# Two weight halves per run of products from the mixing stage on, first-group steps moved, and products of ones at the start of a Trainium2 decoder-layer kernel

## Chip, cores and metric

The kernel runs on one core of one Trainium2 chip. The metric is the device time of one execution in microseconds (us), and a version's time is the median of its runs. The engines are called TensorE (PE, with its weight loads as PEld), VectorE (DVE), ScalarE (ACT), GpSimd (POOL) and SyncE (SP).

## What is computed

One hybrid decoder layer on 256 tokens of width 2048, all in float32. The cut reference:

```python
h = rms_norm(x, norm_mix); proj = h @ w_in            # u, v, q/k/v, z, beta, a, gates
y_a = u * (causal_chunk_mix(rms_norm(v)) + bias)      # gMLP, u and v after GELU
q, k, v = split(silu(causal_conv4(dn_qkv)))
beta, g = sigmoid(dn_beta), -exp(a_log) * softplus(dn_a + dt_bias)
o = gated_delta_rule(q, k, v, g, beta)                # 16 heads of 128, chunked
y_b = rms_norm(o) * silu(z)
merged = gate_a * (y_a @ w_branch_a) + gate_b * (y_b @ w_branch_b)
x = x + merged @ w_out
x = x + (silu(f_gate) * f_up) @ w_down                # SwiGLU, width 5632
x = x + sigmoid(rms_norm(x) @ w_ple_gate) * (p @ w_ple_proj)
return rms_norm(x, norm_final)
```

## The kernel before, in words

**Halves and phases.** All weight matrices are streamed as "halves" of 512 KB (128 x 1024 float32), 604 of them, through rings of four buffers: `raw` as loaded, `whi` (rounded to fp32r) and `wlo` (the rest). A half in feature layout holds 4 k-tiles by 2 column tiles of 128 x 128. For each half, SyncE issues one load (`load_half`, L272, waits until the low part of the half four earlier is made); ScalarE makes the high part (`split_hi`, L278, waits for the load and until the half four earlier is used up, semaphore `half_used`); VectorE makes the low part (`split_lo`, L288); TensorE runs `use_half` (L309). ScalarE and VectorE work three halves ahead (`LEAD`).

**One half on TensorE.** In feature layout the weight is the stationary operand. `use_half` waits for the high part, issues 8 products of 512 columns (`times_high`, L299: high and low activation side by side), waits for the low part and issues 8 products of 256 columns (`times_low`, L304), the last of which counts up `half_used`. In the phases v, proj and most of ple (`rows=True`) the activation is stationary and all products have 512 columns (L319, L324). `gemm` (L584) runs the halves of one output block into one of two accumulators and, through `after`, runs further TensorE steps behind a named half.

**Phases** (`PLAN`, L65): v (16 halves), qkvz (4 head groups of 32 halves, group 0 unrolled, 1 to 3 in a loop), u (16), mix (4 passes of 28; one pass is two blocks of 4, 4, 2 and 4 halves: two gates, branch a, branch b), out (2 passes of 16), ffn (11 passes of 16), down (2 passes of 44, blocks of 11), proj (4), ple (32). The first pass of mix, out, ffn and down is unrolled, the others are loops.

**The written order.** The small work of the delta rule hangs on half numbers, in a table for each engine: `FIRST` for group 0, `START` for the others, `FINISH` for the end of a group, which runs during the next one (TensorE L789 to L792, ScalarE L1120 to L1125, VectorE L1565 to L1571). A step runs behind the half of its number on its engine. Each engine runs its own list in order, so a step that waits holds up the splits or products behind it.

**Group 0.** VectorE scans the log decays (`sum_g`, L1595). ScalarE makes `tails` (L1137, an Exp into `bg`), stores the decays by DMA (`g_store`) and loads them back (`g_load`). TensorE transposes `bg` (`tok_columns`, L608, behind half 2, waits for `tails`); VectorE copies the result (`tok_copy`, L1606), in the middle of which it waits for ScalarE's `tok_exp` (L1142). The keys: two convolution steps (L1424, L1427), `silu_k` on ScalarE (L1019, L1021), `k_columns` on TensorE (L644, behind half 11), normalisation, `gram_m` (L659), `make_negm` (L1492), `store_m` and `load_m` (L1089, L1097, a round trip through DRAM on ScalarE's queue), then GpSimd's `invert` (L484), whose result goes through `store_x` and `load_diag` (L1105, L1113) to `merge32_a` (L701) in the next group. `transpose_k` (L671) and `scale_k` (L1507) must be over before `gram_q` (L680), which reuses their PSUM tile. The v branch ends in `v_norm` and `v_scale` (L1618, L1627).

**First mixing block.** `mix(0)` needs `ya` and `yb` as high and low parts: `ya_high`, `yb_high` on ScalarE (L1223, L1211), `ya_low`, `yb_low` on VectorE (L1692, L1665), placed by the two tables `YS` (L1241, L1708). TensorE waits for both `ya` parts before branch a (L844) and for all four `yb` parts before branch b (L846).

**Start.** TensorE waits for six constants (L621) and the first part of x, ScalarE for `cols` (L1011). Then ScalarE splits x and squares it, GpSimd adds the squares (L475), and TensorE sums them (`first_sum`, L617).

## Time and profile before

| what | value |
|---|---|
| median of 3 runs (lowest, highest) | 1848.9 us (1844.15, 1851.63) |
| profiled execution | 1843.6 us |
| its span, first to last instruction | 1842.0 us |
| mean granted TensorE clock | 0.997 |
| busy: PE, DVE, ACT, POOL | 98%, 64%, 48%, 14% |
| HBM rate over the span | 180 GB/s |

Each instruction row tells its start in us from the start of the span, its duration, the engine (PEld is a weight load, a q behind an engine's name its DMA queue), the line in the kernel, the operation, and the tiles as out<-in with their shapes. Neighbouring equal instructions are merged, with their count as x8. Matmuls overlap, so the spacing of their starts tells their pace and not their duration. A number in brackets is idle time of the engine before the row, with what ended it.

### The profile page before, as it was taken

Reading aid. Unit: us, or ns where it says so; the run is one execution under the profiler, and the core shown is the slowest. Engines: PE = TensorE matmul, PEld = TensorE weight load, DVE = VectorE, ACT = ScalarE, POOL = GpSimd, SP = SyncE. Lnnn points to the kernel's source line nnn. Section 1 sums busy time; section 2 is a strip of 40 time slices with the busy share of each in tenths; the row PEclk is TensorE's granted clock in tenths of the full one; section 3 lists DMA queues with packets and bytes.
Section 4 is the critical chain, followed back from the end, with each engine's and each line's share of the span. In section 5 each row is a group of like instructions: output and inputs, shape, how many; then the busy total and the mean of one; then the engine's idle time right before and its main releaser. Section 6 shows DMA issues by size and latency. Waiting matters only on the chain.

```text
span 1842.0 us, 29968 instructions
## 1 busy us (share of the span) xinstructions
PE 1806.9 (98%) x10742; PEld 1585.7 (86%) x10742; DVE 1177.2 (64%) x1403; ACT 893.3 (48%) x1039; POOL 249.5 (14%) x367
## 2 busy tenths in 40 slices
PE   8899999999999999999999999999999999999998
PEld 6688888888889788888888888888888888888887
DVE  6487697776866656566676655566656555555656
ACT  6645454455455544444444444444444444343455
POOL 4007143070431000000011000000000000000002
PEclk9999999999999999999999999999999999999999
DMA  7455546455465555655555555555555556565653
GB/s 250 139 174 168 159 141 196 123 173 155 150 197 172 182 196 182 194 181 194 172 191 197 193 185 192 183 182 183 190 193 191 189 183 195 183 195 182 217 175 134
DMA packets 103867, 332.94 MB, mean 181 GB/s; under 512 B 23185, under 2 KB 23329, under 8 KB 103521
## 3 DMA queue, kind: packets, MB, share of 16 engines
q1 hardware_dynamic: 88592, 320.57, 53.5%
q10 hardware_dynamic: 14096, 5.07, 1.2%
q0 software_dynamic: 1088, 6.03, 0.9%
q8 instruction: 65, 1.06, 0.2%
q14 instruction: 26, 0.20, 0.0%
HBM read 328.46 MB, written 3.16 MB: 180 GB/s over the span
## 4 chain that ended last, share of the span: by engine, by line
PE 91%; DVE 4%; issue 2%; ACT 2%; DVEq 0%; DMA 0%; ACTq 0%; SPq 0%
PE acc L301 52%; PE acc L306 27%; PE acc L319 4%; PE acc L324 2%; DVE wlo L294 1%; PE ps L635 1%; ACT whi L286 1%; PE acc L901 0%; PE acc L900 0%; PE acc L899 0%; PE ps L687 0%; PE ps L601 0%; PE ps L641 0%; DVE negm L1498 0%; DVE conv_q L1427 0%
## 5 line engine op out<-in xcount | busy, mean ns | idle before, releaser
L294 DVE TENSOR_TENSOR wlo<-raw,whi 128x1024 fp32r<-128x1024 f32 x604 | 755.4, 1268 | 449.2 <-ACT whi L286 445.8
L286 ACT ACTIVATE whi<-raw 128x1024 fp32r<-128x1024 f32 x604 | 625.9, 1055 | 511.1 <-PE acc L306 445.4
L301 PE MATMUL acc<-ax,whi 128*128 128x512 f32 x3072 | 777.9, 395 | 2.9 <-ACT whi L286 2.0
L301 PEld LDWEIGHTS acc<-ax,whi 128*128 128x128 f32 x3072 | 553.3, 189 | 105.4 <-issue 3.0
L306 PEld LDWEIGHTS acc<-ax,wlo 128*128 128x128 f32 x3072 | 419.0, 190 | 30.4
L306 PE MATMUL acc<-ax,wlo 128*128 128x256 f32 x3072 | 428.1, 282 | 0.0
L301 PE MATMUL acc<-fx,whi 128*128 128x512 f32 x704 | 176.3, 392 | 0.0
L301 PEld LDWEIGHTS acc<-fx,whi 128*128 128x128 f32 x704 | 126.6, 189 | 22.6
L967 ACT ACTIVATE t<-acc 128x512 f32<-128x512 f32 x80 | 47.8, 598 | 134.7 <-PE acc L306 131.3
L549 POOL TENSOR_TENSOR sqsum<-sqsum,t 128x512 f32<-128x512 f32 x16 | 22.1, 1381 | 637.6 <-ACT t L1282 637.6
L1395 DVE TENSOR_TENSOR t<-acc,t 128x512 f32<-128x512 f32 x80 | 55.3, 691 | 78.1 <-ACT t L967 77.7
L306 PEld LDWEIGHTS acc<-fx,wlo 128*128 128x128 f32 x704 | 96.0, 190 | 6.9
L306 PE MATMUL acc<-fx,wlo 128*128 128x256 f32 x704 | 98.2, 282 | 0.0
L319 PE MATMUL acc<-whi,ax 128*128 128x512 f32 x320 | 81.9, 399 | 8.3 <-ACT whi L286 8.3
L557 POOL TENSOR_TENSOR t<-t,R 128x512 f32<-128x512 f32 x22 | 28.6, 1298 | 451.7 <-ACT t L1295 451.7
L493 POOL TENSOR_TENSOR blk_t<-blk_m,blk_x 128x60 f32<-128x60 f32 (+24 forms) x124 | 58.4, 471 | 173.9 <-DMA blk_m<-inv_in 164.6
L319 PEld LDWEIGHTS acc<-whi,ax 128*128 128x128 f32 x320 | 61.2, 193 | 21.0 <-issue 8.2
L495 POOL TENSOR_TENSOR blk_x<-blk_x,blk_t 128x60 f32<-128x60 f32 (+24 forms) x124 | 70.0, 565 | 9.7
L301 PE MATMUL acc<-yb,whi 128*128 128x512 f32 x256 | 64.2, 393 | 1.9 <-DVE yb L1668 1.9
L301 PE MATMUL acc<-mx,whi 128*128 128x512 f32 x256 | 64.1, 392 | 0.0
L301 PEld LDWEIGHTS acc<-yb,whi 128*128 128x128 f32 x256 | 46.0, 189 | 10.3 <-DVE yb L1668 2.1
L301 PEld LDWEIGHTS acc<-mx,whi 128*128 128x128 f32 x256 | 46.0, 189 | 8.2
(269 smaller groups left out, 1366.8 us busy)
## 6 DMA issues: line engine op xcount, KB each, us to landing
raw<-in_win SPq DMA_DIRECT2D x224, 512.0 KB, 3.6
raw<-in_wgu SPq DMA_DIRECT2D x176, 512.0 KB, 4.1
raw<-in_wd SPq DMA_DIRECT2D x88, 512.0 KB, 4.1
raw<-in_wb SPq DMA_DIRECT2D x32, 512.0 KB, 4.2
raw<-in_wo SPq DMA_DIRECT2D x32, 512.0 KB, 4.3
raw<-in_wpg SPq DMA_DIRECT2D x32, 512.0 KB, 3.9
raw<-in_wa SPq DMA_DIRECT2D x16, 512.0 KB, 4.6
blk_m<-inv_in ACTq DMA_DIRECT2D x16, 128.0 KB, 3.0
```

Source lines behind the costliest of these rows:

```text
L286: nc.scalar.activation(whi[:, s], raw[:, s], ACT.Copy).then_inc(hi_done, 1)
L294: nc.vector.tensor_tensor(wlo[:, s], raw[:, s], whi[:, s].bitcast(F32), ALU.subtract).then_inc(lo_done, 1)
L301: nc.tensor.matmul(o, whi[:, s, kt, m * P:(m + 1) * P], x[:, k].rearrange("p q n -> p (q n)"), start=begin, stop=False, skip_group_check=True)
L306: return nc.tensor.matmul(o[:, 0:SEQ], wlo[:, s, kt, m * P:(m + 1) * P], x[:, k, 0], start=False, stop=end, skip_group_check=True)
L319: nc.tensor.matmul(into[buf][:, m], x[:, WIDE_K * h + kt, q, m * P:(m + 1) * P], whi_w[:, s, kt], start=first and kt == 0 and q == 0, stop ...
L324: mm = nc.tensor.matmul(into[buf][:, m], x[:, WIDE_K * h + kt, 0, m * P:(m + 1) * P], wlo_w[:, s, kt], start=False, stop=last and kt == WI ...
L493: chain(g.tensor_tensor(tmp, blk_m[:, j + 1:32, j:j + 1].to_broadcast([P, r, c]), blk_x[:, j:j + 1, 0:c].to_broadcast([P, r, c]), ALU.mult ...
L495: chain(g.tensor_tensor(blk_x[:, j + 1:32, 0:c], blk_x[:, j + 1:32, 0:c], tmp, ALU.add), v + 3 + 2 * j)
L549: g.tensor_tensor(sqsum[:], sqsum[:], piece(t[1], q % 2), ALU.add).then_inc(s["added"], 1)
L557: g.tensor_tensor(piece(t[1], j), piece(t[0], j), over(R[:], 2), ALU.mult).then_inc(ff_gate, 1)
L967: f(dst, accv[buf][:, :, 1], ACT.Copy).then_inc(low_taken, 1)
L1395: v.tensor_tensor(dst, accv[buf][:, :, 0], dst, ALU.add).then_inc(part_summed, 1)
```

## The change

It has four parts.

1. `use_pair` and `gemm_pairs`: two halves per run, high products of both (16), then low products of both (16). They are used in all of mix but three blocks of its first pass, and in the loop passes of out, ffn and down. Blocks with an odd number of halves end with a single one.
2. Group 0: `tok_columns` from half 2 to 5, `gram_q` from 22 to 23, `q_columns` from 24 to 25, `transpose_v` from 27 to 28; on ScalarE `tails` from 2 to 3, `tok_exp` from 4 to 6, the root for v from 6 to 8; on VectorE `tok_copy` from 3 to 6, `v_scale` from 7 to 9.
3. First mixing block: the first high and low part of `yb` are made in phase u, the others and those of `ya` one place earlier, and TensorE waits for each part of `ya` and `yb` just ahead of the half that reads it.
4. Start: 16 products of 64 columns of ones on TensorE, ahead of all else, and a Copy of one column of ones on ScalarE ahead of its wait for `cols`.

```diff
+WARM = 16
+    def use_pair(pe, phase, i, n, buf, first, last, h, x):
+        for p in range(2):
+            pe.wait_ge(hi_done, half_of(phase, i, n + p) + 1)
+            for kt in range(HALF_K):
+                for m in range(2):
+                    times_high(acc[buf][:, m], (n + p) % RING, kt, m, x, HALF_K * (h + p) + kt, first and p == 0 and kt == 0)
+        for p in range(2):
+            pe.wait_ge(lo_done, half_of(phase, i, n + p) + 1)
+            for kt in range(HALF_K):
+                for m in range(2):
+                    mm = times_low(acc[buf][:, m], (n + p) % RING, kt, m, x, HALF_K * (h + p) + kt,
+                                   last and p == 1 and kt == HALF_K - 1)
+            mm.then_inc(half_used, 1)
...
+            def gemm_pairs(phase, i, n0, halves, buf, use, x):
+                acc_free(pe, phase, i, buf, use)
+                for n in range(0, halves - 1, 2):
+                    use_pair(pe, phase, i, n0 + n, buf, n == 0, n + 2 == halves, n, x)
+                if halves % 2:
+                    use_half(pe, phase, i, n0 + halves - 1, buf, False, True, halves - 1, x)
...
+            pe.wait_ge(consts_made, 1)
+            for n in range(WARM):
+                mm(psf[1][:, 64 * n:64 * n + 64], ones[:], ones[:, 0:64], start=True, stop=True)
             pe.wait_ge(consts_made, 6)
...
-            FIRST = {2: tok_columns, 11: k_columns, 14: k_rows, 16: gram_m, 19: transpose_k, 22: gram_q, 24: q_columns, 27: transpose_v}
+            FIRST = {5: tok_columns, 11: k_columns, 14: k_rows, 16: gram_m, 19: transpose_k, 23: gram_q, 25: q_columns, 28: transpose_v}
...
             def mix(i, after=None):
                 for b in range(2):
-                    gemm("mix", i, MIX * b, HID, 0, 2 * b, ax, after=after if b == 0 else None)
-                    gemm("mix", i, MIX * b + HID, HID, 1, 2 * b, ax)
-                    pe.wait_ge(ya_lo, 2)
-                    gemm("mix", i, MIX * b + 2 * HID, HGM, 0, 2 * b + 1, ya)
-                    pe.wait_ge(yb_lo, NGROUPS)
-                    gemm("mix", i, MIX * b + 2 * HID + HGM, HID, 1, 2 * b + 1, yb)
+                    if after and b == 0:
+                        gemm("mix", i, MIX * b, HID, 0, 2 * b, ax, after=after)
+                    else:
+                        gemm_pairs("mix", i, MIX * b, HID, 0, 2 * b, ax)
+                    gemm_pairs("mix", i, MIX * b + HID, HID, 1, 2 * b, ax)
+                    if after and b == 0:
+                        pe.wait_ge(ya_lo, 1)
+                        gemm("mix", i, 2 * HID, HGM, 0, 1, ya, after={0: operand_ready(ya_lo, 2)})
+                        pe.wait_ge(yb_lo, 1)
+                        gemm("mix", i, 2 * HID + HGM, HID, 1, 1, yb, after={h: operand_ready(yb_lo, h + 2) for h in range(HID - 1)})
+                    else:
+                        gemm_pairs("mix", i, MIX * b + 2 * HID, HGM, 0, 2 * b + 1, ya)
+                        gemm_pairs("mix", i, MIX * b + 2 * HID + HGM, HID, 1, 2 * b + 1, yb)
...
-                    gemm("out", i, b * HID, HID, b % 2, b // 2, mx)
+                    gemm_pairs("out", i, b * HID, HID, b % 2, b // 2, mx)
...
-                    gemm("ffn", i, b * HID, HID, b % 2, b // 2, ax)
+                    gemm_pairs("ffn", i, b * HID, HID, b % 2, b // 2, ax)
...
-                    gemm("down", i, b * HFF, HFF, b % 2, b // 2, fx)
+                    gemm_pairs("down", i, b * HFF, HFF, b % 2, b // 2, fx)
...
+            act.wait_ge(consts_made, 1)
+            f(preload[:, 0:1], ones[:, 0:1], ACT.Copy)
             act.wait_ge(cols_in, 16)
...
                 if n == 2:
+                    g_store(0)
+                if n == 3:
                     tails()
-                    g_store(0)
                 if n == 4:
-                    tok_exp()
                     g_load(0)
                 if n == 6:
+                    tok_exp()
+                if n == 8:
                     act.wait_ge(v_mean, 3)
                     f(vrms[:], vrms[:], ACT.Sqrt).then_inc(v_root, 1)
...
+                if n == 14:
+                    yb_high(0)
...
-            YS = {0: (lambda: yb_high(0),), 1: (lambda: yb_high(1),), 2: (lambda: yb_high(2),), 5: (lambda: ya_high(0),),
+            YS = {0: (lambda: yb_high(1),), 1: (lambda: yb_high(2),), 5: (lambda: ya_high(0),),
                   6: (lambda: ya_high(1),), 7: (lambda: yb_high(3),)}
...
-                if n == 3:
+                if n == 6:
                     tok_copy()
...
-                if n == 7:
+                if n == 9:
                     v_scale()
...
                     o_scale(NGROUPS - 1)
+                    yb_low(0)
...
-            YS = {0: (lambda: yb_low(0),), 1: (lambda: norm_o(NGROUPS - 1),), 2: (lambda: yb_low(1),), 3: (sv_bias,),
-                  4: (lambda: ya_mult(0), lambda: ya_mult(1)), 6: (lambda: ya_low(0),), 7: (lambda: ya_low(1),),
-                  8: (lambda: yb_low(2),), 9: (lambda: yb_low(3),)}
+            YS = {0: (lambda: yb_low(1),), 1: (lambda: norm_o(NGROUPS - 1),), 3: (sv_bias,),
+                  4: (lambda: ya_mult(0), lambda: ya_mult(1)), 5: (lambda: ya_low(0),), 6: (lambda: ya_low(1),),
+                  7: (lambda: yb_low(2),), 8: (lambda: yb_low(3),)}
```

## Rows read from the trace of the kernel before

**Rows 1.** The page: the span, and each engine's busy time.
```profile
span 1842.0 us, 29968 instructions
PE 1806.9 (98%) x10742; PEld 1585.7 (86%) x10742; DVE 1177.2 (64%) x1403; ACT 893.3 (48%) x1039; POOL 249.5 (14%) x367
```

**Rows 2.** Waits of TensorE: who waited for whom, us in total, times, longest.
```profile
...
PE ps L614 <- ACT bg L1140: 7.3, 1, 7.3
PE ps L687 <- DVE kbeg L1510: 2.6, 1, 2.6
...
PE acc L301 <- DVE ya L1694: 1.9, 1, 1.9
PE acc L301 <- DVE yb L1668: 1.9, 1, 1.9
...
```

**Rows 3.** Timeline, 70 to 84 us: ScalarE and TensorE around the gate transposes.
```profile
...
76.37 1.06 ACT L286 ACTIVATE whi<-raw 128x1024 fp32r<-128x1024 f32 x1
...
78.74 0.40 ACT L1140 ACTIVATE bg<-bg 16x128 f32<-16x128 f32 x1
...
79.45 3.52 PE L301 MATMUL acc<-ax,whi 128*128 128x512 f32 x8
...
```

**Rows 4.** Timeline, 85 to 107 us: the chain to the key lengths.
```profile
...
85.98 0.69 DVE L1395 TENSOR_TENSOR pre<-acc,pre 128x512 f32<-128x512 f32 x1
...
99.76 2.46 DVE L1427 SCALAR_TENSOR_TENSOR conv_k<-pre,cols,conv_k 128x256 f32<-128x256 f32 x6
...
104.25 1.06 ACT L1021 ACTIVATE t<-conv_k 128x1024 f32<-128x1024 f32 x1
...
106.10 1.84 PE L635 MATMUL ps<-ones,t 128*128 128x1 f32 x16
...
```

**Rows 5.** Timeline, 128 to 146 us: the chain to the query gram.
```profile
...
128.30 2.15 DVE L1498 SCALAR_TENSOR_TENSOR negm<-ps,tok,negm 128x128 f32<-128x128 f32 x8
...
135.91 1.74 ACTq L1102 DMA_DIRECT2D blk_m<-inv_in  x4
...
145.80 2.02 PE L687 MATMUL ps<-conv_q,kn 128*128 128x128 f32 x16 [2.63 <-DVE kbeg L1510]
...
```

**Rows 6.** Timeline, 178 to 193 us: from GpSimd's inversion to the first merge.
```profile
...
178.17 1.48 POOL L497 COPY blk_xT<-blk_x 128x256 f32<-128x256 f32 x1 [0.17 <-POOL blk_x L495]
...
181.32 2.65 ACTq L1110 DMA_DIRECT2D inv_out<-blk_xT  x4
...
188.74 0.41 ACTq L1117 DMA_DIRECT2D diagT<-inv_out  x1
...
192.29 1.09 PE L709 MATMUL ps<-diagT,negm 32*32 32x32 f32 x32
...
```

**Rows 7.** Timeline of VectorE in the first mixing block: the first low part of ya.
```profile
...
605.46 1.22 DVE L1694 TENSOR_TENSOR ya<-ytmp,ya 128x1024 fp32r<-128x1024 f32 x1
...
```

**Rows 8.** Timeline of TensorE in ffn: one half and the start of the next.
```profile
...
1201.51 2.00 PE L301 MATMUL acc<-ax,whi 128*128 128x512 f32 x8
1203.35 1.11 PE L306 MATMUL acc<-ax,wlo 128*128 128x256 f32 x8
1204.30 2.00 PE L301 MATMUL acc<-ax,whi 128*128 128x512 f32 x8
...
```

**Rows 9.** Timeline of TensorE in ple, where every product has 512 columns.
```profile
...
1772.33 1.98 PE L319 MATMUL acc<-whi,ax 128*128 128x512 f32 x8
1774.14 1.07 PE L324 MATMUL acc<-wlo,ax 128*128 128x512 f32 x4
...
```

**Rows 10.** Timeline of the first 36 us: the cold start and what paces it.
```profile
...
8.25 3.75 PE L319 MATMUL acc<-whi,ax 128*128 128x512 f32 x8 [8.25 <-ACT whi L286]
...
33.90 3.88 ACT L286 ACTIVATE whi<-raw 128x1024 fp32r<-128x1024 f32 x4
...
35.67 1.98 PE L319 MATMUL acc<-whi,ax 128*128 128x512 f32 x8
...
```

**Rows 11.** The page: the costliest group, VectorE's low parts.
```profile
...
L294 DVE TENSOR_TENSOR wlo<-raw,whi 128x1024 fp32r<-128x1024 f32 x604 | 755.4, 1268 | 449.2 <-ACT whi L286 445.8
...
```

More of the change, by code:

```diff
@@ L838, in _, with operand_ready @@
                 gemm("u", 0, p * HID, HID, p % 2, p // 2, ax, after=last_steps(p * HID, HID))
+            def operand_ready(done, last):
+                return lambda: pe.wait_ge(done, last)
             def mix(i, after=None):
                 for b in range(2):
-                    gemm("mix", i, MIX * b, HID, 0, 2 * b, ax, after=after if b == 0 else None)
-                    gemm("mix", i, MIX * b + HID, HID, 1, 2 * b, ax)
-                    pe.wait_ge(ya_lo, 2)
-                    gemm("mix", i, MIX * b + 2 * HID, HGM, 0, 2 * b + 1, ya)
-                    pe.wait_ge(yb_lo, NGROUPS)
-                    gemm("mix", i, MIX * b + 2 * HID + HGM, HID, 1, 2 * b + 1, yb)
+                    if after and b == 0:
[11 more added lines that the diff above has]
+                        gemm_pairs("mix", i, MIX * b + 2 * HID + HGM, HID, 1, 2 * b + 1, yb)
             mix(0, after={0: lambda: turn_o(NGROUPS - 1), 2: spatial})
@@ L851, in _ @@
                 mix(i)
-            def operand_ready(done, last):
-                return lambda: pe.wait_ge(done, last)
             pe.wait_ge(mix_lo, 6)
```

## The prediction

> **What bounds the kernel now.** I read the page first. TensorE is busy for 1806.9 of 1842.0 us [rows 1], and no other engine comes near, so time is won only where TensorE waits or where its products come further apart than they need to. The waits of TensorE come second: four of them touch this change, 7.3, 2.6, 1.9 and 1.9 us [rows 2], 13.7 us together. Then the timelines around each, to see what is late next, and last the pace in the long loops. There a half takes 2.79 us, 1.84 for its 8 wide products and 0.95 for its 8 narrow ones [rows 8]. That is 0.230 and 0.119 us a product. Where wide products follow wide ones, 8 take 1.81 us, 0.226 each [rows 9]. So a wide run behind a narrow one costs some 0.025 us more than its products.
>
> **Part 1, two halves per run.** Nothing is added or removed; 159 pairs are formed (51 in mix, 8 in out, 80 in ffn, 20 in down). Each pair has one turn from narrow to wide less.
> - Gain: 0.025 us per pair, 4.0 us in all. Against it, the first narrow product behind a wide one may be quicker than the others: at 0.12 each, 8 would take 0.96 and they take 0.95 [rows 8]; a pair loses that once, up to 0.01. That leaves 0.015, or 2.4 us.
> - Bounds: 0.025 a pair (4.0 us) if the turn alone costs. If a narrow run of twice the length leaves twice the loss behind it, the turn costs the same per half and only the 0.01 is left, 1.6 us slower. I take 2.4, since the loss in rows 8 stands in the first products behind the turn and I see it as a fixed cost.
> - What hides the rest: in a pair `half_used` of the first half comes at 2 x 1.84 + 0.95 = 4.63 us instead of 2.79, so ScalarE may write that ring slot 1.84 us later. Its split (1.06) and VectorE's (1.27 [rows 11]) start three halves, 8.4 us, ahead. Tightest are the loops of out and down, where VectorE does two adds, a product and a low part (0.69 each [rows 4]) at each block's end and ScalarE two more operations, all ahead of the next split. Worked through from the end of a block: split and low part of the late slot until 1.5 us after it, three VectorE steps to 3.8, two of ScalarE's to 5.1, the split to 6.1; TensorE asks for it at 5.57 + 1.84 = 7.4. 1.3 us of cover stay. SyncE's loads wait for the same low parts and have a half more.
>
> *By a page.* In the Trainium skill, "TensorE: Matmul & The Clock Gate", section "Back-to-back issue gap", the spacing follows from the column count alone, with a small constant. By that rule order costs nothing and this part gives 0 instead of 2.4 us. The trace does not quite agree (0.230 against 0.226 for the same 512 columns).
>
> **Part 2, group 0.** This carries most of the sum, and its chain has four steps.
> - *The gate transposes.* TensorE ends half 2 at 71.8 us, waits 7.3 us for `tails`, which ends at 78.74 + 0.40 = 79.1, and then runs at the lower of its two clock levels (1.2 GHz): 8 wide products take 3.52 instead of 2.00 us [rows 3, 8]. That is 7.3 + 1.5 = 8.8 us. Behind half 5 the step comes 3 x 2.79 = 8.4 us later, at 80.2; `tails` is put behind one more split, so it ends at 80.1. Half 5 needs the split that ends at 77.4 [rows 3] and would start at 77.4. Both just fit: 8.8 us are free so far.
> - *The key lengths*, not moved, are late next. VectorE works from 85.98 to 102.2 without a gap up to the second key convolution, ScalarE's square ends at 105.3 and TensorE starts at 106.1 [rows 4]: 0.8 us of slack against 8.8 of advance. But the chain moves too. VectorE's stretch can begin when ScalarE has copied the first block, right behind `tails`: 80.1 + 0.6, so at 80.9. It loses `v_scale` (some 1.4 us, two passes of 1024 columns, which is what a low part is by size) and gets the token copies with their wait for `tok_exp` (some 1.6, being about ten short steps): 16.4 us instead of 16.2, so it ends at 97.3. ScalarE's two passes take it to 99.6. TensorE gets there at 97.3 and waits 2.3 us; a wait of 2.6 [rows 5] is followed by products at full pace, so the clock stays. Gain here: 106.1 - 99.6 = 6.5 us.
> - *The query gram.* From there on VectorE has no gap to close and stays 5.6 us ahead of before, TensorE 6.5. The chain `make_negm`, store, load, query SiLU, low parts to `scale_k` [rows 5] moves by 5.6. One half later, TensorE asks for it 2.8 us later: 2.8 - 0.9 = 1.9 of the 2.6 us go, 8.4 in all. `q_columns` and `transpose_v` only follow, one half later, at their old price.
> - *The inversion.* It starts with `load_m` [rows 5], so GpSimd too is 5.6 us early and ends at 179.65 - 5.6 = 174.0. ScalarE would store the result at 181.3 - 8.4 = 172.9 and now waits for it until 174.1, 7.2 us earlier than before; the DMA round trip to the first merge (181.3 to 192.3 [rows 6]) keeps its 11 us, and behind the waiting ScalarE stand its splits and block copy, so VectorE comes no earlier either. The gain falls to 7.3 us and is kept, since everything behind is paced by TensorE.
>
> Part 2 gives 7.3 us; its bounds are 8.4 (the inversion hidden) and 2.6 (the key chain doesn't move: 0.7 there and 1.9 at the gram).
>
> **Part 3, first mixing block.** Both waits are 1.9 us [rows 2]. The first `ya` part is ready at 605.46 + 1.22 = 606.7 [rows 7]; a weight's low part and the second `ya` part follow, some 2.3 us more, to 609.0, which is 1.9 behind TensorE: it wants `ya` at 607.1 and the second part only a half later. In the new order both come one low part earlier. Of `yb` the first is ready in phase u, the second and third long before, the fourth is wanted three halves later. The restart behind each wait goes with it, some 0.1 us. Cover: ScalarE and VectorE, for which nothing but order changes. Gain 4.0 us, bounds 3.8 and 4.2.
>
> **Part 4, start.** The first 8 wide products take 3.75 instead of 1.98 us [rows 10], at the lower clock level. If the products of ones lift the clock, TensorE is early, but it soon waits: ScalarE's split that ends at 33.9 + 1.05 = 34.95, itself paced by GpSimd's adds, feeds the products of 35.67 [rows 10]. So the gain is 0 to 0.7 us. The ones end some 4 us ahead of the first real product, which speaks against it; I take 0.3. The Copy brings ScalarE's table load forward, under the wait for the first weights: nothing.
>
> **Sum.** 2.4 + 7.3 + 4.0 + 0.3 = 14.0 us, or 1843.6 - 14.0 = 1829.6 us for the profiled execution. That one lies 5.3 us under the median of 1848.9, so I predict 1848.9 - 14.0 = 1834.9 us. What a measurement of this kernel can tell from no change is about 0.5%, 9.2 us.
>
> **The rivals.**
> - *The wait moves over.* The key chain doesn't come forward (ScalarE stuck in `tok_exp` behind VectorE, and VectorE in the same stretch as before). For it: 0.8 us of slack now, and VectorE with no gap from 86 to 102 us [rows 4]. Against it: VectorE's stretch starts when ScalarE lets it, and that is 5 us earlier. Part 2 gives 2.6, the sum 9.3, the time 1839.6 us. 19%, half of it under the bound of 9.2.
> - *The pairs give nothing.* By rows 8 and 9 this is a matter of 0.015 us a pair, close to the resolution of the rows. Sum 11.6, time 1837.3 us; with the loss of 1.6, 1838.9. 18%. This is the page's rule above.
> - *The pairs starve TensorE: slower.* Place: the split behind each block's end, where 1.3 us of cover stay. If ring slots freed 1.84 us later, with two loads bunched, make it late, TensorE waits once in each of the 77 paired blocks. It decides once the delay passes 1.3 + 14.0 / 77 = 1.5 us; at 1.3 + 0.3 it costs 23 us, and the time is 1848.9 - 14.0 + 23.1 = 1858.0 us. For it: the ring has only four slots. Against it: no wait in these loops is among TensorE's now [rows 2], and splits and low parts fill 2.3 of a half's 2.8 us on two engines. 6%.
> - *Nothing visible.* The median of other executions lies elsewhere than the profile, by up to 5 us, and small losses add up: sum 6 us, time 1842.9. 7%.
>
> **How the numbers follow.** My forecast has 50%, its own range 1831 to 1838. The range of 8 in 10 reaches from the best case (4.0 + 8.4 + 4.2 + 0.7 = 17.3 us, with some scatter of the median: 1829.0) to the case with 6 us gained, 1843.0. Faster by over 0.5%: nearly all of the forecast (47 of 50), 15 of the second rival's 18 and 9 of the first's 19 points: 71 of 100, which I take down to 66 for scatter of both medians. Slower by over 0.5%: 6. Within: 28.
>
> **What would show it.** Right: no wait at the gate transposes, and one of 2 to 3 us in front of the key-length products (L635) with `silu_k`'s square just ahead; the first merge in group 1 some 7 us earlier than 192.3; no waits for `ya` and `yb`; in the loops 16 wide and 16 narrow products per 5.57 us instead of 5.59. Wrong: a wait of over 6 us at the key lengths, pairs that take 5.59 us or more, any wait for `whi` in out, ffn or down, or a new wait in front of the first merges that eats more than 2 us.

## The result and the profile after

| what | before | changed |
|---|---|---|
| median (lowest, highest) | 1849.99 us (1844.15, 1851.63), 4 runs | 1826.07 us (1825.33, 1826.44), 4 runs |
| ratio, 95% interval | | 0.9883 (0.9870 to 0.9896) |
| profiled execution, span | 1843.6, 1842.0 us | 1825.33, 1823.7 us |

The change takes 1.2% off (1.1% in a later set, below). The direction was right, the forecast of 1834.9 us too small a gain, and the result lies 2.9 us below the range of 1829.0 to 1843.0.

The page of the changed kernel, its first lines and two of its queues:

```profile
span 1823.7 us, 30031 instructions
...
PE 1807.9 (99%) x10774; PEld 1590.6 (87%) x10774; DVE 1165.3 (64%) x1403; ACT 884.2 (48%) x1040; POOL 251.4 (14%) x367
...
q1 hardware_dynamic: 88592, 320.57, 54.0%
...
q8 instruction: 48, 0.79, 0.2%
...
```

TensorE has 32 more instructions of each kind than in [rows 1]: each of the 16 products of ones is recorded as two. The last line matters later. It is the queue that the page calls "instruction": it brings the program's own code, in 48 loads of some 16 KB (0.79 MB / 48). The page of before has 65 there.

The waits of TensorE in the changed kernel, which answer to [rows 2]:

```profile
PE ps L646 <- POOL ones L465: 1.2, 1, 1.2
PE acc L320 <- ACT whi L287: 1.0, 2, 0.7
PE ps L661 <- ACT t L1056: 1.0, 1, 1.0
PE ps L856 <- DVE oT L1601: 1.0, 1, 1.0
PE acc L302 <- ACTq L1192: 0.9, 1, 0.9
...
PE ps L760 <- DVE invT L1564: 0.6, 1, 0.6
...
```

All four waits of [rows 2] are gone. Three of about 1 us stand for them: ahead of half 4 of group 0 (L302, ACTq), at the key lengths (L661), and a new one in the first mixing block (L856).

To see where the time came from, take the start of the same step in both traces and subtract. A difference that stays the same from one step to the next means that nothing happened between them.

| step on TensorE | before, us | changed, us | gained so far | the part |
|---|---|---|---|---|
| end of stage v (first beta product) | 47.56 | 47.71 | -0.15 | start |
| key lengths | 106.10 | 99.59 | 6.51 | group 0 |
| first merge, group 1 | 192.29 | 183.80 | 8.49 | group 0 |
| first merge, group 2 | 308.07 | 298.40 | 9.67 | in no part |
| first merge, group 3 | 424.90 | 412.99 | 11.91 | in no part |
| first merge, in u | 539.50 | 527.58 | 11.92 | |
| second block of the first mixing pass | 628.00 | 612.87 | 15.13 | mixing order |
| proj | 1729.45 | 1711.17 | 18.28 | pairs |
| end | 1841.96 | 1823.70 | 18.26 | |

So by the traces: start -0.2, group 0 8.6, mixing order 3.2, pairs 3.1. With the start counted in, these are 14.8 us, against the 14.0 forecast. The other 3.4 us are gained between the merges of groups 1 and 3, where the change alters not one instruction. There TensorE goes from the last half of a pass of the loop of groups to the first half of the next. In before, the timeline of TensorE around the two back jumps shows:

```profile
291.13 2.10 PE L301 MATMUL acc<-ax,whi 128*128 128x512 f32 x8 [0.93 <-issue]
...
407.95 2.10 PE L301 MATMUL acc<-ax,whi 128*128 128x512 f32 x8 [1.96 <-ACT whi L286]
...
```

and in the changed kernel the halves at the second back jump follow each other every 2.8 us:

```profile
401.72 2.00 PE L302 MATMUL acc<-ax,whi 128*128 128x512 f32 x8
403.56 1.12 PE L307 MATMUL acc<-ax,wlo 128*128 128x256 f32 x8
404.52 2.00 PE L302 MATMUL acc<-ax,whi 128*128 128x512 f32 x8
406.36 1.11 PE L307 MATMUL acc<-ax,wlo 128*128 128x256 f32 x8
407.31 2.00 PE L302 MATMUL acc<-ax,whi 128*128 128x512 f32 x8
...
```

A back jump is where TensorE goes from the end of the loop's body to its start. The time from one first merge to the next holds one of them: 115.8 us (group 1 to 2) and 116.8 (2 to 3) in before, 114.6 for both in the changed kernel.

**Group 0.** The changed kernel at the gate transposes (L637) and the key lengths (L661), the answer to [rows 3, 4]:

```profile
75.76 2.14 PE L302 MATMUL acc<-ax,whi 128*128 128x512 f32 x8 [0.88 <-ACTq L1192]
...
79.85 0.40 ACT L1175 ACTIVATE bg<-bg 16x128 f32<-16x128 f32 x1
...
80.91 0.69 DVE L1434 TENSOR_TENSOR pre<-acc,pre 128x512 f32<-128x512 f32 x1 [0.93 <-ACT pre L1000]
...
81.46 0.30 PE L637 MATMUL ps<-ident,bg 80*128 80x80 f32 x2
81.54 1.69 PEld L302 LDWEIGHTS acc<-ax,whi 128*128 128x128 f32 x8
81.56 2.08 PE L302 MATMUL acc<-ax,whi 128*128 128x512 f32 x8
...
94.89 2.46 DVE L1466 SCALAR_TENSOR_TENSOR conv_k<-pre,cols,conv_k 128x256 f32<-128x256 f32 x6
...
98.48 1.06 ACT L1056 ACTIVATE t<-conv_k 128x1024 f32<-128x1024 f32 x1
...
99.59 1.95 PE L661 MATMUL ps<-ones,t 128*128 128x1 f32 x16 [1.03 <-ACT t L1056]
...
```

`tails` ends at 80.25, just ahead of the transposes, and the wide products keep the higher clock level (2.08 us for 8, against 3.52). VectorE's stretch begins at 80.91 and ends at 97.35, the square at 99.54.

The query gram, and the end of the inversion with its way to the first merge, in the same kernel (to [rows 5, 6]):

```profile
135.76 0.26 POOL L509 TENSOR_TENSOR blk_t<-blk_m,blk_x 128x31 f32<-128x31 f32 x1 [95.61 <-DMA blk_m<-inv_in]
...
140.08 2.02 PE L713 MATMUL ps<-conv_q,kn 128*128 128x128 f32 x16
...
175.29 0.70 POOL L513 COPY blk_xT<-blk_x 128x256 f32<-128x256 f32 x1 [0.17 <-POOL blk_x L511]
...
176.10 2.69 ACTq L1145 DMA_DIRECT2D inv_out<-blk_xT  x4
...
180.88 0.41 ACTq L1152 DMA_DIRECT2D diagT<-inv_out  x1
...
183.65 1.39 POOL L518 COPY invT<-diagT 32x256 f32<-32x256 f32 x1 [7.66 <-DMA diagT<-inv_out]
...
```

The store now leaves 0.1 us after GpSimd's last copy, so it is GpSimd that sets it. From the store to the merge at 183.80 it is 7.7 us, not the 11.0 of [rows 6]. In before ScalarE stood idle for 4.19 us until the store had landed, issued the load at 188.74, and went on with this row:

```profile
189.34 0.60 ACT L967 ACTIVATE pre<-acc 128x512 f32<-128x512 f32 x1 [4.19 <-DMA inv_out<-blk_xT]
```

**Mixing and the long loops.** The first block of the mixing stage in the changed kernel (to [rows 7, 8]), then four runs of products in ffn:

```profile
578.53 3.81 PE L856 MATMUL ps<-gmw,xT 128*128 128x128 f32 x32 [0.98 <-DVE oT L1601]
...
596.11 2.00 PE L302 MATMUL acc<-ya,whi 128*128 128x512 f32 x8
...
601.70 2.00 PE L302 MATMUL acc<-yb,whi 128*128 128x512 f32 x8
...
```

```profile
1191.08 2.08 PE L307 MATMUL acc<-ax,wlo 128*128 128x256 f32 x16
1192.99 3.82 PE L302 MATMUL acc<-ax,whi 128*128 128x512 f32 x16
1196.65 2.08 PE L307 MATMUL acc<-ax,wlo 128*128 128x256 f32 x16
...
```

No wait for `ya` or `yb` is left. A pair takes 1196.65 - 1191.08 = 5.57 us: 1.91 for the narrow run, 3.66 for the wide one.

### The profile page after: what moved, and what is told of

Read it like the earlier page. It is cut to its first block, busy times and chain, and to the rows that moved or that the text cites. A ratio compares the mean times of both kernels' runs of the same rounds, so it can differ in the third digit from the quotient of the medians.

```text
span 1823.7 us, 30031 instructions
## 1 busy us (share of the span) xinstructions
PE 1807.9 (99%) x10774; PEld 1590.6 (87%) x10774; DVE 1165.3 (64%) x1403; ACT 884.2 (48%) x1040; POOL 251.4 (14%) x367
## 4 chain that ended last, share of the span: by engine, by line
PE 83%; issue 7%; DVE 4%; POOL 3%; DMA 1%; ACT 1%; DVEq 0%; ACTq 0%; POOLq 0%; SPq 0%
PE acc L302 49%; PE acc L307 25%; PE acc L320 3%; PE acc L325 1%; DVE wlo L295 1%; POOL blk_x L511 1%; POOL blk_t L509 1%; DMA raw<-in_win 1%; POOL sqsum L491 1%; PE ps L661 1%; PE acc L934 0%; PE acc L933 0%; PE acc L932 0%; ACT whi L287 0%; DVE negm L1537 0%
## 5 line engine op out<-in xcount | busy, mean ns | idle before, releaser
L302 PE MATMUL acc<-ax,whi 128*128 128x512 f32 x3072 | 755.6, 394 | 1.0 <-ACTq L1192 0.9
L302 PEld LDWEIGHTS acc<-ax,whi 128*128 128x128 f32 x3072 | 559.1, 188 | 109.2 <-issue 1.7
L307 PEld LDWEIGHTS acc<-ax,wlo 128*128 128x128 f32 x3072 | 404.4, 191 | 21.9 <-DVE wlo L295 0.2
L307 PE MATMUL acc<-ax,wlo 128*128 128x256 f32 x3072 | 411.0, 282 | 0.0
L302 PE MATMUL acc<-fx,whi 128*128 128x512 f32 x704 | 172.5, 391 | 0.0
L302 PEld LDWEIGHTS acc<-fx,whi 128*128 128x128 f32 x704 | 127.9, 189 | 23.7
L509 POOL TENSOR_TENSOR blk_t<-blk_m,blk_x 128x60 f32<-128x60 f32 (+24 forms) x124 | 68.0, 548 | 166.7 <-DMA blk_m<-inv_in 157.2
L511 POOL TENSOR_TENSOR blk_x<-blk_x,blk_t 128x60 f32<-128x60 f32 (+24 forms) x124 | 64.1, 517 | 9.7
L302 PE MATMUL acc<-mx,whi 128*128 128x512 f32 x256 | 62.6, 391 | 0.0
L302 PE MATMUL acc<-yb,whi 128*128 128x512 f32 x256 | 61.4, 391 | 0.0
L302 PEld LDWEIGHTS acc<-yb,whi 128*128 128x128 f32 x256 | 46.9, 188 | 9.0
L302 PEld LDWEIGHTS acc<-mx,whi 128*128 128x128 f32 x256 | 46.5, 189 | 8.7
```

The source lines that it names most:

```text
L302: nc.tensor.matmul(o, whi[:, s, kt, m * P:(m + 1) * P], x[:, k].rearrange("p q n -> p (q n)"), start=begin, stop=False, skip_group_check=True)
L307: return nc.tensor.matmul(o[:, 0:SEQ], wlo[:, s, kt, m * P:(m + 1) * P], x[:, k, 0], start=False, stop=end, skip_group_check=True)
L509: chain(g.tensor_tensor(tmp, blk_m[:, j + 1:32, j:j + 1].to_broadcast([P, r, c]), blk_x[:, j:j + 1, 0:c].to_broadcast([P, r, c]), ALU.mult ...
L511: chain(g.tensor_tensor(blk_x[:, j + 1:32, 0:c], blk_x[:, j + 1:32, 0:c], tmp, ALU.add), v + 3 + 2 * j)
```

## The experiments

Each part was tried alone on the kernel before, three of the four were taken out alone from the changed kernel, and what was left over was chased by moving TensorE's code. Ratios are to the kernel before on the same chip, whose median there was 1846.48, 1845.78 and 1845.87 us in the three sets; it was the reference in each.

**The kernel before with the ones alone**

```diff
+            pe.wait_ge(consts_made, 1)
+            for n in range(WARM):
+                mm(psf[1][:, 64 * n:64 * n + 64], ones[:], ones[:, 0:64], start=True, stop=True)
             pe.wait_ge(consts_made, 6)
...
+            act.wait_ge(consts_made, 1)
+            f(preload[:, 0:1], ones[:, 0:1], ACT.Copy)
```

> The kernel before with the 16 products of ones and the Copy alone. Theory A (place of the code): the two stalls of TensorE of 0.9 and 2.0 us at the back jumps of the head-group loop, with instruction loads in every pass, come from where the loop's code lies; the ones shift it, so both stalls and the loads during passes 2 and 3 vanish: profile some 3 us shorter than 1842.0, median 3 to 9 us below before. Rival B (timing): the stalls go because TensorE comes to the loop earlier in the changed kernel; then this kernel keeps both stalls and the loads, and its time is within 1 us of before.

1840.95 us (1839.36 to 1844.12, 11 runs), ratio 0.9972 (0.9963 to 0.9981). The page counts the instruction loads; over 280 to 400 us, where the first back jump lies, the queues of the kernel before carry this last line:

```profile
q8 instruction: 10, 0.16, 0.6%
```

and those of the kernel with ones this one:

```profile
q8 instruction: 1, 0.02, 0.0%
```

Over the whole span it has 48 loads, and none between the one at 280.5 and the one at 531.2 us. Its first product starts at 8.27 us, after 16 products that ran from 1.19 on:

```profile
1.19 7.09 PE L624 MATMUL ps<-ones 128*128 128x64 f32 x32 [1.19 <-POOL ones L450]
8.27 3.74 PE L320 MATMUL acc<-whi,ax 128*128 128x512 f32 x8
...
```

The start gives 0.26 us by the end of stage v. The gain comes later: -0.5 at group 1, +0.7 at group 2, +2.9 at group 3, and unchanged to the end. So 16 products that compute nothing pay off 290 and 410 us later, at the back jumps. The median gains more than this one pair of traces shows, 5 us by the ratio.

**The kernel before with the first group's steps alone** (the lines of part 2 of the change, and no others)

> The kernel before with the moved steps of group 0 alone. All theories: no 7.3 us wait, first merge of group 1 8 us earlier. Theory A: the back-jump stalls stay, since no instruction is added ahead of the loop; profile 1842.0 - 8.5 = 1833.5, median some 8.5 us below before. Rival B: the stalls go too, profile near 1830. Rival C (the lottery sits in the 7.3 us wait and the low clock behind it): the median falls by 13 us or more.

1837.44 us (1835.46 to 1841.11, 5 runs), ratio 0.9953 (0.9939 to 0.9966), 65 loads. In the trace 7.46 us are gained at group 1's first merge; 4.58 at group 2's and 2.49 at group 3's are left. Stalls of 2.26 and 2.52 us stand at the back jumps, both put down to `whi`, and behind each the granted clock is at the lower level for 3.4 us (285.34 to 288.75, 404.81 to 408.22). The moved steps earn what they should by group 1, and in the execution profiled, the slowest of the five, the back jumps take 5 us of it away. TensorE comes to them 7.5 us earlier than in before and stalls all the same, so it is not the earlier arrival that frees them.

**The kernel before with the pairs alone** (`use_pair`, `gemm_pairs` and their calls)

> The kernel before with two halves per run alone, all other waits as before. Fixed cost of the turn: 159 pairs by 0.017 us, 2.7 us shorter. Cost that doubles with the length of the narrow run: within 1 us of before. Starving: waits for whi in out, ffn or down and a longer time.

1845.81 us (1842.1 to 1851.95, 11 runs), ratio 0.9996 (0.9986 to 1.0006), 65 loads: by the median, nothing. I had expected 2.7 us. The trace is clearer. It was 4.4 us late by group 1's first merge, ahead of any pair. From the second block of the first mixing pass to proj it goes from 5.29 us late to 2.15, and that is 3.14 us for the pairs. This stretch hardly varies: it took 1101.443 us in each of the seven profiled executions without pairs, before among them, and 1098.303 in each of the seven with pairs. No wait for `whi` stands in any of the loops with pairs.

**The kernel before with the first mixing block alone** (the `mix` waits, `yb_high(0)`, `yb_low(0)` and the two `YS` tables)

> The kernel before with the operands of the first mixing block at their new places alone. The two waits of 1.9 us go; if they are won in full, 4.0 us shorter; if the wait of 1.0 us ahead of the spatial products, which the changed kernel has and the one before has not, is the price of making the first part of yb in phase u, 3.0 to 3.3 us shorter, and that wait is seen here too.

1842.12 us (1840.58 to 1847.4, 11 runs), ratio 0.9982 (0.9972 to 0.9991), 65 loads. TensorE's waits of this kernel have no line for `ya` or `yb`, and a new one:

```profile
PE acc L302 <- ACT whi L287: 4.0, 2, 2.0
...
PE ps L849 <- DVE oT L1590: 1.0, 1, 1.0
...
```

From the merge in u to the second mixing block it gains 3.17 us (from -3.02 to +0.15). The first line is the back jumps again, 2.0 each, here without a fall of the clock behind them.

**The changed kernel again, and without its ones**

```diff
-            pe.wait_ge(consts_made, 1)
-            for n in range(WARM):
-                mm(psf[1][:, 64 * n:64 * n + 64], ones[:], ones[:, 0:64], start=True, stop=True)
...
-            act.wait_ge(consts_made, 1)
-            f(preload[:, 0:1], ones[:, 0:1], ACT.Copy)
```

> The changed kernel once more, beside the runs of the kernel before on this chip, where their median is now 1846.5 us over 27 runs. The theory that the parts add (group 0 some 9, place of the code 5, first mixing block 4, pairs 2.7) gives 1846.5 - 20.7 = 1826 us, with a scatter of about 1 us, since no back-jump stall is left. If the 1850 of the first comparison was the true level of before, the ratio stays at 0.988.

> The changed kernel without the products of ones and the Copy. Place of the code: 65 instruction loads instead of 48, stalls of 2 us and more at both back jumps of the group loop, a low clock behind the longer ones, and 5 to 10 us longer than the changed kernel, with wide scatter. Rival (the ones only warm the clock): within 1 us of the changed kernel, 48 loads.

Again: 1825.86 us (1824.29 to 1830.73, 6 runs), ratio 0.9893 (0.9875 to 0.9910), 48 loads. Without ones: 1830.01 us (1829.69 to 1833.01, 6 runs), ratio 0.9914 (0.9898 to 0.9931), 65 loads. Two stalls are back, the second of them in this row:

```profile
400.52 2.11 PE L302 MATMUL acc<-ax,whi 128*128 128x512 f32 x8 [1.62 <-issue]
...
```

The first is 0.76 us at 283.79. The ones are worth 4.2 us in the medians, where I had expected 5 to 10 and longer stalls. Of the 4.45 us between the two profiled executions 3.2 lie between the merges of groups 1 and 3 and 1.3 ahead of group 1, where a split came late at 138 us. Nor did this kernel scatter widely: its six runs lie within 3.3 us, those of the changed kernel beside it within 6.4.

**The kernel before with 64 semaphore increments at TensorE's start**

```diff
+            for n in range(64):
+                pe.sem_inc(waits_carried, 1)
             pe.wait_ge(consts_made, 6)
```

> The kernel before with 64 semaphore increments at the start of TensorE's program instead of products of ones: instructions that only move the code behind them. Place of the code: as with the ones alone, 48 instruction loads, no back-jump stall, median 5.5 us below before. Rival (warm clock or the products themselves): as before, 65 loads and both stalls.

1844.46 us (1842.46 to 1845.58, 12 runs), ratio 0.9985 (0.9973 to 0.9996); 48 loads, none from 283.2 to 532.4. The increments do no work, and the back jumps are free: from group 1 to group 3 it gains 3.4 us (-1.66 to +1.74). But I had expected a median 5.5 us below before, and it gains 1.3, or 2.8 by the ratio. The trace shows two prices. At the start the first product comes at 10.92 us instead of 8.25, and 1.2 us of that are left at the end of stage v. And behind the loop the first merge in u waits 0.4 us for the load of the inverse. Trace against trace it ends 1.8 us behind the kernel with the ones. The medians of the two differ by more (1840.95 and 1844.46, in two sets), and what makes up the rest wasn't found.

**The same 64 increments at TensorE's end**

```diff
                 last.then_inc(ple_tile, 1)
+            for n in range(64):
+                pe.sem_inc(waits_carried, 1)
```

> The kernel before with 64 semaphore increments on TensorE's queue behind its last product: the same added instructions as in the run that put them at the start, but no instruction ahead of the loops is moved. Theory A (what counts is where the loop of groups lies, and with it what must be loaded at its back jumps): 65 instruction loads, gaps of 0.9 to 2.5 us at both back jumps, ratio 1.000 within its interval. Rival (the length of the program, or the draw of one build against another, moves the time): ratio 0.9985 or lower, as with the increments at the start.

1846.9 us (1843.94 to 1854.24, 12 runs), ratio 1.0003 (0.9993 to 1.0013), 65 loads. TensorE's timeline has stalls again at both back jumps:

```profile
297.10 3.35 PE L301 MATMUL acc<-ax,whi 128*128 128x512 f32 x7 [2.79 <-issue]
```

and 1.55 and 0.63 us at 416.23 and 421.31. The program is as long as with the increments in front, and it gains nothing. What counts is where the loop lies. The execution profiled was the slowest of the twelve.

**The changed kernel with 33 increments for its ones**

```diff
-                mm(psf[1][:, 64 * n:64 * n + 64], ones[:], ones[:, 0:64], start=True, stop=True)
+                pe.sem_inc(waits_carried, 1)
```

(33 times, ahead of the wait for six constants; ScalarE's Copy is out too.)

> The changed kernel with its 16 products of ones (and ScalarE's Copy) replaced by 33 semaphore increments on TensorE's queue, in the same place: about as many instructions, no work. Theory A (the ones are worth only the shift they give to the code behind them): 48 instruction loads, none in the loop of groups, no gap at its back jumps, and a median within 1 us of the changed kernel, 1825.5 to 1827. Rival (the products themselves matter, by the clock of the first products or in another way): 1828 to 1830, as without the ones, even where the loads are gone. If 33 increments are not enough of a shift, 65 loads and 1830, and nothing is decided.

1838.09 us (1835.71 to 1840.87, 6 runs), ratio 0.9959 (0.9945 to 0.9972), 65 loads. I had counted 32 instructions for the ones, and they are 64 (32 products, 32 weight loads), so the shift was half as large. It made things worse: TensorE now stalls twice at each back jump. The second one:

```profile
402.81 1.65 PE L302 MATMUL acc<-ax,whi 128*128 128x512 f32 x6 [0.52 <-issue]
407.63 1.01 PE L302 MATMUL acc<-ax,whi 128*128 128x512 f32 x2 [3.17 <-issue]
408.44 1.91 PE L307 MATMUL acc<-ax,wlo 128*128 128x256 f32 x8
...
```

The stalls sum to 1.24 + 2.13 + 0.52 + 3.17 = 7.1 us. Behind the longer one of each pair the clock is low for 3.4 us (8 narrow products take 1.91 instead of 1.11 us), and a wait of 0.9 for VectorE stands at 245.8. In all 11.8 us are lost from group 1 to group 3, against the kernel with ones. With the same 65 loads, no ones at all cost 3.2 there. So the number of loads does not give the price. That it depends on where in the stream of products each one falls is a guess that no run tests. This run doesn't decide whether the ones have a value of their own. The starts say that what they give there is small: stage v ends at 46.91 to 47.71 us in the six profiled executions with ones, 47.28 on average, and at 47.27 to 47.62 in the seven with neither ones nor 64 increments ahead of it, 47.46 on average.

**The changed kernel without its pairs, and without its steps of group 0**

```diff
                 acc_free(pe, phase, i, buf, use)
-                for n in range(0, halves - 1, 2):
-                    use_pair(pe, phase, i, n0 + n, buf, n == 0, n + 2 == halves, n, x)
-                if halves % 2:
-                    use_half(pe, phase, i, n0 + halves - 1, buf, False, True, halves - 1, x)
+                gemm(phase, i, n0, halves, buf, use, x)
```

(there in place of the whole body of `gemm_pairs`; in the second kernel all lines of part 2 of the change are turned back.)

> The changed kernel with its pairs undone: all halves run singly again, the other three parts stay. Theory A (a pair saves 0.020 us, 5.57 against 5.59, whatever stands beside it; the rest is the place of the code): it loses 3.1 us between the first mixing pass and the proj stage in the traces, has no back-jump stalls as long as the instruction loads inside the loop of groups stay away (48), and its median is 1829 us. Rival (the pairs gain also by what they do to the code's length or to the loops' stalls, as the 20 us of the medians would allow): 1832 us or more, with loads back in the loop of groups or new gaps in the loops behind it.

> The changed kernel with the first group's steps where they stood before; pairs, mixing order and ones stay. Theory A: the first merge of group 1 comes 8 to 8.5 us later than in the changed kernel, nothing later gives it back, and the median is 1826 + 8.5 = 1834.5 us (1833.5 to 1836). Rival (the two waits were partly paid for by something downstream, such as GpSimd's chain or the load clock, so that moving the steps is worth less than the traces say): 1829 to 1832. In either case 48 instruction loads and no gap at the loop's back jumps.

Without pairs: 1829.49 us (1827.55 to 1830.98, 5 runs), ratio 0.9910 (0.9896 to 0.9923). Without the steps: 1834.57 us (1833.66 to 1837.4, 5 runs), ratio 0.9940 (0.9927 to 0.9953). Both have 48 loads and no stall at the back jumps. In the trace the first loses 3.14 us from the second mixing block to proj, as much as the pairs alone gained. The second is 8.33 us behind at the first merge of group 1 and 8.32 and 8.33 at the next two, then 9.1 at the merge in u, which waits 0.7 us for the load of the inverse. Waits of 7.3 and 2.6 us are back.

**The changed kernel with `yb_low(0)` behind half 2 of mix**, a try at a better version

```diff
                     o_scale(NGROUPS - 1)
-                    yb_low(0)
...
-            YS = {0: (lambda: yb_low(1),), 1: (lambda: norm_o(NGROUPS - 1),), 3: (sv_bias,),
+            YS = {1: (lambda: norm_o(NGROUPS - 1),), 2: (lambda: yb_low(0), lambda: yb_low(1)), 3: (sv_bias,),
```

> The changed kernel with the first low part of yb made behind half 2 of the mixing stage, with the second, instead of behind the last half of phase u. If it is what makes norm_o late, the wait of 1.0 us ahead of the spatial products goes and the kernel is 1.0 us faster than the changed one; if it makes the parts of ya late instead, a wait ahead of branch a takes its place and the time is the same.

1825.03 us (1824.18 to 1826.83, 5 runs), ratio 0.9883 (0.9866 to 0.9900). The spatial products now follow without a wait:

```profile
578.31 1.28 DVE L1601 SCALAR_TENSOR_TENSOR oT<-ps,cols,oT 128x1024 f32<-128x1024 f32 x1
...
580.10 3.07 PE L856 MATMUL ps<-gmw,xT 128*128 128x128 f32 x26
...
```

`ya` and `yb` have no waits either. Against the changed kernel it gains 0.9 us from the merge in u to the second mixing block. The medians agree with that (0.8 us), but the intervals overlap, so the gain is shown by that stretch of the trace alone. The whole execution profiled, the slowest of the five, was 1.5 us longer than the changed kernel's, with a fall of the clock behind the key lengths.

**Do the parts add up?** Taken out one at a time, against 1825.86: pairs 3.6, group 0 8.7, ones 4.2. Pairs and group 0 ran in another set, whose median of before was 0.1 us off. Mixing order was not taken out; its trace shows 3.2. The sum is 19.7 us, and the whole is 1845.78 - 1825.86 = 19.9. Put in one at a time, by their ratios: ones 5.2, group 0 8.7, mixing 3.3, pairs 0.7, together 17.9. The sets differ by 1 us on the ones, and on the pairs, for which the traces of both show 3.14.

## Why the forecast was right in its parts and wrong in its sum

Two steps of the prediction failed. Its sum put the waits of TensorE at the loop's back jumps at nothing, because no step stands there that the change moves; the runs show 3.4 us gained there, by where the added instructions put the loop. And it carried an offset of 5.3 us from profile to median over to a kernel in which it is 0.7. Both are worked out below, behind the four parts.

**Pairs: right, a little too small.** Forecast 2.4, measured 3.1. A pair's period is 5.567 us (median over ffn), two single halves take 2 x 2.793 = 5.586, and 3.14 us over 157 pairs is 0.020 each. The loss is fixed per turn, as assumed: in a pair the first five wide products come 228 to 236 ns apart and the rest 227. Both terms were mis-sized a little, the same way: a turn costs 0.027 us where 0.025 was taken, and a narrow run starts 0.008 us early, lost once a pair, where 0.01 was taken. Both bounds were right, and so was the cover: no wait for a weight. By the Trainium skill, "TensorE: Matmul & The Clock Gate", section "Back-to-back issue gap", spacing depends on the column count and this part gives 0. The trace does not agree: the first wide products behind narrow ones are up to 9 ns late (236 against 227), and three microseconds hang on it.

**Group 0: the keys and the gram as forecast, the inversion not.** The key lengths came at 99.59 (forecast 99.6), 6.5 us early. TensorE reached them later than thought, so it waited 1.0 there and 0.9 at half 4, in place of 2.3 at once. The query gram gained 5.72 + 2.79 = 8.5 (forecast 8.4). The inversion did not clip the gain to 7.3. "The DMA round trip keeps its 11 us" is what failed here. The load goes out when the store has landed, 7.4 us behind the store in before and 4.8 in the changed kernel: the last of the store's four transfers took 5.3 us to land in before and 2.7 now. And the merge follows the load in 2.9 us instead of 3.55. That made up for GpSimd, which began 5.6 us early as forecast but ended only 3.7 early (175.99 against 179.65). The merge came 8.5 us early, just over the upper bound of 8.4. But neither number is fixed. From the first store to the landing of the load it takes 6.5 to 10.2 us in the seven profiled executions with moved steps and 10.3 to 10.7 in the others, and no run shows what makes it short. The first merge of group 1 came 6.4 to 8.8 us earlier than in before in those seven, 7.7 on average, so 8.5 is one value of several, and 7.3 lies among them. It is near its limit: the kernel without pairs waits 0.4 us there for the load. One assumption of this part held only by luck of the execution profiled, that a wait at the key lengths leaves the clock up. In the second execution of the changed kernel the clock is low from 102.37 to 105.78, in the kernel with `yb_low(0)` moved from 100.23 to 107.05. From the key lengths to the gram they take 0.9 and 2.4 us longer than the 40.5 of the first one. The clock fell there in four of the seven profiled executions with moved steps. (The prediction's 7.3 holds a slip of 0.1: the store comes 181.3 - 174.1 = 7.2 us earlier.)

**Mixing: right but for a wait that I created.** Both waits of 1.9 went (forecast gain 4.0, measured 3.2, under the lower bound of 3.8). "Nothing but order changes" overlooked who waits for VectorE's moved work: `yb_low(0)` (1.22 us) stands ahead of `norm_o`, and the spatial products wait for that. 1.0 us was given back. The experiment that moved it took the wait away.

**Start: small, as forecast, but the account was wrong.** The ones did not end 4 us ahead of the first real product. Recorded as 32 products of 0.22 us each, they ran to 8.28. The first real product moved from 8.25 to 8.64, the last 0.36 us of it a wait for its split; with the ones alone it came at 8.27. The clock rose at 11.12 to 13.62 us in the six profiled executions with ones (11.44 in the first of the changed kernel) and at 10.88 to 14.26 in the seven with neither ones nor 64 increments ahead (14.26 in before), so the ones did not decide it. The -0.15 of the table is scatter of the start; by the averages above the ones give 0.2 us by the end of stage v, where 0.3 was forecast. TensorE then waited 0.7 us for the split that feeds the products of [rows 10], as forecast.

**What was missing: the back jumps, and with them the offset.** The forecast missed by 1834.9 - 1826.1 = 8.8 us, in two nearly equal halves. The sum against the profiled execution was 4.3 us short (1829.6 against 1825.3). 3.4 of that are the two stalls at the back jumps, 2.9 with 0.5 of restart. The other 0.9 is what is left of four misses that partly cancel: group 0 1.3 too low, pairs 0.7 too low, mixing 0.8 and start 0.4 too high. That they cancel is luck. The stalls stood among the waits of the kernel before, 2.0 for `whi` and 0.9 for "issue", and I read only the four waits at steps that are moved. Adding instructions ahead of a loop is an edit to the loop.

The other 4.5 us are the offset: I took the 5.3 us between the profile and the median as fixed, and in the changed kernel it is 0.7. Part of that offset was the same thing. The profile of before had stalls of 0.9 and 2.0 us; other kernels with 65 loads had up to 2.3 and 2.5, or 2.8 and 2.2, some with a fall of the clock behind them. Of the kernels with many runs, those with 65 loads range over 9.1 us (the kernel before, 17 runs) and 10.3 (increments at the end, 12), those with 48 over 4.8 (ones alone, 11) and 3.1 (increments in front, 12). In the smaller sets around the changed kernel the ranges do not sort this way (3.3 us with 65 loads, up to 6.4 with 48). A second part may lie at a wait that the change removes: at the query gram of [rows 5] the clock fell in three of the seven profiled executions that wait there (2.98, 3.15 and 3.29 us) and not in the others (2.24 to 2.78, before among them). And a third part was the small sample, or the chip: in the later sets of 17 to 27 runs the kernel before has a median of 1845.8 to 1846.5 us, so that the profiled 1843.6 lies 2.2 to 2.9 below it, not 5.3, and the whole change is worth 19.9 us there (ratio 0.9893) instead of 23.9.

**The rivals.** The wait that moves over to the key lengths did not come (1.0 us, not over 6). Pairs that give nothing, and pairs that starve TensorE, fall by the traces of all seven kernels with pairs: the long stretch is 3.14 us shorter in each, without a wait. "Nothing visible" falls by the result.

**What stays open.** That the loads cause the stalls rests on the seven profiled executions with 48 loads, none of which has a stall at a back jump, against the seven with 65, all of which have one at each, and on two placements of the same 64 instructions. From first merge to first merge, group 1 to 2 and 2 to 3, the fourteen times are 114.56 to 114.62 us with 48 loads and 115.8 to 120.9 with 65; from group 3 to u, with no back jump between, all seven kernels with 65 loads take 114.6. That the time of a load is what makes a stall long or short was read from no view. Why one placement needs no loads in the later passes and another does was not tried: no run varied the shift in small steps. Nor was it tried whether the ones have a value beyond their shift; that the increments in front gained less in the median leaves room for one. What made the transfers of the inverse's store land sooner is open too.

## What to carry to other kernels

If the trace shows code being loaded inside a loop from its second pass on, with gaps at the back jump put down to "issue" or to a split that had long been there, try some instructions in front of the loop before tuning anything in it, and look at the loads again; a shift can also make it worse (against the changed kernel without ones, the ones gave 4 us and 33 increments cost 8). Take an offset between profile and median as a thing with causes, which a change can remove. And when work is moved forward on an engine, ask what stands behind it there, as well as who waits for it.

## What the runs showed of the hardware

- **Code placement.** 64 instructions without effect ahead of TensorE's loops took the instruction loads from 65 to 48 and 3.4 us of stalls and restarts away; behind the last product they did nothing; 33 in front of the changed kernel, in place of its ones, cost 11.5 us in the trace and 12 in the medians. In before 18 loads lie between 288 and 518 us, in the second and third pass of the loop of groups; in the changed kernel none lies between 273.2 and 522.1.
- **A short stall can cost twice.** At the five gaps of 2.1 to 3.2 us at the back jumps the granted clock fell to its lower level, for 3.4 us, and for 6.8 at the 2.79 of the increments at the end. At 0.9 and 2.0 in before, 2.0 and 2.0 in the first mixing block alone, and 0.8 and 1.6 in the changed kernel without ones, it did not. At the wait of 1.0 for the key lengths it fell in four of the seven profiled executions that have it.
- **Turns between shapes.** 512-column products behind 256-column ones start 228 to 236 ns apart for the first five, then 227.
- **Long loops without waits repeat to the nanosecond.** From the second mixing block to proj it took 1101.443 us in seven profiled executions and, with pairs, 1098.303 in seven others.
- **Small float32 products.** A 64-column product of ones is recorded as two of 0.22 us each, at the start where the clock is low.
